# Two halves of the adaLN sums, h modulated on ScalarE, two projection tiles in turn

## What is computed

```python
mod = silu(c) @ ada_w + ada_b                      # c: 1024, ada_w: 1024 x 3072
shift, scale, gate = split(mod, 3)
h = rmsnorm(x, norm_g) * (1.0 + scale) + shift     # x: 1024 x 1024, f32
z = h @ w_in                                       # 1024 x 2760
xr, gr, q, k, v, ga, qi, ki, wi = split(z)
y_r = rg_lru(conv(xr)) * silu(gr)                  # 512 channels
y_a = dsa_attention(q, k, v, qi, ki, wi) * silu(ga)   # index scores, top 256 keys per query
x = x + gate * (concat(y_r, y_a) @ w_out)
out = rmsnorm(x, final_g)
```

## Time and profile before

| | |
|---|---|
| median of 3 runs | 621.33 us (620.89 to 621.44) |
| the profiled execution's own time | 619.93 us |
| its span, first to last instruction | 618.1 us |
| mean granted TensorE clock | 0.926 of full |
| busy: TensorE, VectorE, ScalarE, GpSimd | 87%, 71%, 61%, 38% of the span |

### The profile page before, as it was taken

How to read it: one execution, slowest core, us unless ns; L and a number is a source line. 1 busy time by engine, 2 the same in 40 slices (tenths; PEclk the granted TensorE clock), 3 DMA queues, 4 the chain that set the end, 5 groups by cost and what they waited for, 6 DMA issues and landing times.

```text
span 618.1 us, 8029 instructions
## 1 busy us (share of the span) xinstructions
PE 535.4 (87%) x2676; PEld 444.8 (72%) x2676; DVE 439.5 (71%) x992; ACT 377.4 (61%) x679; POOL 233.5 (38%) x195
## 2 busy tenths in 40 slices
PE   1459989998999999999999526489999999999994
PEld 1346868777787777778888415478889999888873
DVE  5987386885999889898697886854475666664522
ACT  6513236453499999987898555554466666656531
POOL 5150862352344274677642003740402030313322
PEclk9859999998999999999999855569999999999999
DMA  8967342430112111135550420110011000101011
GB/s 335 418 206 266 105 118 53 102 85 18 36 34 69 34 36 34 35 103 137 140 133 0 177 96 0 68 36 2 8 61 43 28 36 34 41 30 69 0 69 68
DMA packets 16457, 51.96 MB, mean 84 GB/s; under 512 B 4000, under 2 KB 5024, under 8 KB 15392
## 3 DMA queue, kind: packets, MB, share of 16 engines
q1 hardware_dynamic: 16416, 51.45, 26.3%
HBM read 37.81 MB, written 4.19 MB: 68 GB/s over the span
## 4 chain that ended last, share of the span: by engine, by line
PE 68%; DVE 11%; DMA 7%; POOL 5%; ACT 4%; issue 3%; SPq 2%; DVEq 0%; POOLq 0%; ACTq 0%
PE pair L1373 30%; PE pair L1470 13%; PE pair L1492 6%; PE pair L1505 5%; DMA ada<-in_ada_w 4%; PE pair L1448 3%; PE pair L1449 2%; DMA qs<-half_lo 2%; PE pair L1422 2%; DVE rank L1156 2%; PE pair L1514 2%; PE pair L1413 2%; PE pair L1414 2%; DVE tie L1158 1%; POOL half_lo L726 1%
## 5 line engine op out<-in xcount | busy, mean ns | idle before, releaser
L1373 PE MATMUL pair<-h_hi,w_hi 128*128 128x512 f32 (+1 forms) x352 | 114.4, 407 | 1.6 <-DVE h_lo L1064 1.5
L1373 PE MATMUL pair<-h_lo,w_hi 128*128 128x512 f32 (+1 forms) x352 | 109.8, 393 | 0.0
L1373 PE MATMUL pair<-h_hi,w_lo 128*128 128x512 f32 (+1 forms) x352 | 109.0, 391 | 0.0
L1298 DVE TENSOR_TENSOR pt_lo<-pair,pt_hi 128x512 fp32r<-128x512 f32 (+3 forms) x96 | 50.5, 554 | 71.1 <-ACT pt_hi L963 70.5
L858 ACT ACTIVATE bias_sb<-score_sb,tinies 128x1024 bf16<-128x1024 f32 (+2 forms) x93 | 95.7, 1032 | 3.2 <-DVE tinies L1109 3.1
L696 POOL TENSOR_SCALAR w_hi<-w_raw 128x1024 fp32r<-128x1024 f32 (+1 forms) x22 | 29.4, 1339 | 136.3 <-PE pair L1373 120.5
L1373 PEld LDWEIGHTS pair<-h_hi,w_hi 128*128 128x128 f32 (+1 forms) x352 | 65.0, 188 | 19.0 <-issue 6.2
L1373 PEld LDWEIGHTS pair<-h_lo,w_hi 128*128 128x128 f32 (+1 forms) x352 | 66.0, 188 | 15.5 <-issue 0.8
L1373 PEld LDWEIGHTS pair<-h_hi,w_lo 128*128 128x128 f32 (+1 forms) x352 | 65.6, 186 | 15.4 <-issue 0.7
L1095 DVE TENSOR_SCALAR_CACHE_REDUCE bias_sb<-score_sb,tinies 128x640 bf16<-128x640 f32 (+2 forms) x93 | 72.6, 802 | 0.9
L781 POOL TENSOR_TENSOR x_res<-q_free,x_res 128x512 f32<-128x512 f32 x14 | 18.1, 1296 | 121.0 <-DVE q_free L1269 121.0
(11 more groups left out here) (195 smaller groups left out, 1254.2 us busy)
## 6 DMA issues: line engine op xcount, KB each, us to landing
w_raw<-in_w_tiles SPq DMA_DIRECT2D x21, 512.0 KB, 3.5
ada<-in_ada_w SPq DMA_DIRECT2D x8, 1024.0 KB, 18.4
x_sb<-in_x SPq DMA_DIRECT2D x8, 512.0 KB, 7.1
ada_g<-in_ada_w SPq DMA_DIRECT2D x8, 512.0 KB, 4.5
qs<-half_hi SPq DMA_DIRECT2D x16, 256.0 KB, 3.6
qs<-half_lo SPq DMA_DIRECT2D x16, 256.0 KB, 4.4
wo_raw<-in_w_out SPq DMA_DIRECT2D x8, 512.0 KB, 6.4
x_res<-in_x SPq DMA_DIRECT2D x8, 512.0 KB, 3.3
```

Of the source, the lines that this page charges most:

```text
L1298: nc.vector.tensor_tensor(pt_lo[:, 4 * b:4 * b + nc4, hh, :], psum[use % 2][:, 0:nc4 * P].rearrange("p (c q) -> p c q", q=P), f32(pt_hi[:, ...
L1373: ins = nc.tensor.matmul(psum[banks[half]][0:width, :], w[b][:, k, 0:width], hh[:, k, half * HALF:(half + 1) * HALF], start=(k == 0 and p ...
```

## The change

`MOD_GROUPS` becomes two equal halves of the channel chunks, 0 to 3 and 4 to 7, and everything up to h follows them.

- SP loads slab 0, then for all eight row chunks the columns of the first half (shift and scale, 2 x 512 columns, 512 KB), then slab 1, then the same for the second half. That is sixteen loads in place of eight, with rows of 2 KB in place of 8 KB.
- VectorE sums the first half (8 operations over 1024 elements), two of the second, forms shift and scale of the first, sums two more, and then takes `low_half(k)` and a sum in turn; then shift and scale of the second half and four more `low_half`.
- ScalarE modulates: h_hi directly from `xt` with Identity, bias and scale, then `xt` in place.
- TensorE does the first column sums, then ksteps of tile 0 and tile 1 in turn for each chunk, with the second column sums ahead of chunk 3.
- `FIRST_US` goes from 46 to 37.

```diff
-MOD_GROUPS = [(0, 3), (3, KC)]
+MOD_GROUPS = [(0, KC // 2), (KC // 2, KC)]
-FIRST_US = 46.0
+FIRST_US = 37.0
...
-            for k in range(KC):
-                sp.dma_start(ada[k][:, :], ada_w[k * P:(k + 1) * P, 0:2 * D]).then_inc(ada_in[k], 16)
-                if k >= KC - 2:
-                    load_slab(k - (KC - 2))
+            for n in range(2):
+                load_slab(n)
+                for k in range(KC):
+                    src = ada_w[k * P:(k + 1) * P, 0:2 * D].rearrange("p (b m) -> p b m", b=2)
+                    sp.dma_start(ada[k][n][:, :, :], src[:, :, n * (D // 2):(n + 1) * (D // 2)]).then_inc(ada_in[k][n], 16)
...
             for k in range(KC):
-                act.wait_ge(h_full, k + 1)
-                nc.scalar.activation(h_hi[:, k, :], xt[:, k, :], ACT.Copy).then_inc(h_hi_ok, 1)
+                act.wait_ge(mod_ok, k // (KC // 2) + 1)
+                act.wait_ge(xt_act, 2 * KC)
+                shift, scale = mod[:, k:k + 1], mod[:, 8 + k:9 + k]
+                nc.scalar.activation(h_hi[:, k, :], xt[:, k, :], ACT.Identity, bias=shift, scale=scale).then_inc(h_hi_ok, 1)
+                act.wait_ge(h_hi_ok, k + 1)
+                nc.scalar.activation(xt[:, k, :], xt[:, k, :], ACT.Identity, bias=shift, scale=scale).then_inc(h_full, 1)
...
+            def accumulate(k, n):
+                g0, g1 = MOD_GROUPS[n]
+                v_acc = acc[:, :].rearrange("p (b m) -> p b m", b=2)[:, :, g0 * P:g1 * P]
+                dve.wait_ge(ada_in[k][n], 16)
+                if k == 0:
+                    dve.wait_ge(c_ok, 1)
+                    nc.vector.tensor_scalar(v_acc, ada[k][n][:, :, :], c_act[:, k:k + 1], None, ALU.mult).then_inc(acc_ok[n], 1)
+                else:
+                    dve.wait_ge(acc_ok[n], k)
+                    nc.vector.scalar_tensor_tensor(v_acc, ada[k][n][:, :, :], c_act[:, k:k + 1], v_acc, ALU.mult, ALU.add).then_inc(acc_ok[n], 1)
+            def modulation(n):
+                g0, g1 = MOD_GROUPS[n]
+                dve.wait_ge(mod_ps, n + 1)
...
+            def low_half(k):
+                dve.wait_ge(h_full, k + 1)
+                nc.vector.tensor_tensor(h_lo[:, k, :], xt[:, k, :], f32(h_hi[:, k, :]), ALU.subtract).then_inc(h_lo_ok, 1)
             for k in range(KC):
...
+                accumulate(k, 0)
+            accumulate(0, 1)
+            accumulate(1, 1)
+            modulation(0)
+            accumulate(2, 1)
+            accumulate(3, 1)
+            for k in range(KC // 2):
+                low_half(k)
+                accumulate(KC // 2 + k, 1)
+            modulation(1)
+            for k in range(KC // 2, KC):
+                low_half(k)
...
+            mod_sums(0)
             for k in range(KC):
-                kstep(0, k)
-                if k >= KC // 2:
-                    kstep(1, k - KC // 2)
-            for k in range(KC // 2, KC):
-                kstep(1, k)
+                if k == KC // 2 - 1:
+                    mod_sums(1)
+                for j in range(2):
+                    kstep(j, k)
```

More of the change, by code:

```diff
@@ L351, in layer_kernel @@
         R_H = region(65536)
-        ada = [sb(f"ada{k}", R_H + 8192 * k, [P, 2048]) for k in range(KC)]
+        ada = [[sb(f"ada{k}_{n}", R_H + 32768 * (k // 4) + 16384 * n + 4096 * (k % 4), [P, 2, D // 2]) for n in range(2)] for k in range(KC)]
         h_hi = sb("h_hi", R_H, [P, KC, S], F32R)
@@ L479, in layer_kernel @@
         x_in = [sem(f"x_in{t}") for t in range(NT)]
-        ada_in = [sem(f"ada_in{k}") for k in range(KC)]
+        ada_in = [[sem(f"ada_in{k}_{n}") for n in range(2)] for k in range(KC)]
         w_in_s = [sem(f"w_in{b}") for b in range(2)]
@@ L496, in layer_kernel @@
         mod_ps = sem("mod_ps")
-        acc_ok = sem("acc_ok")
+        acc_ok = [sem(f"acc_ok{n}") for n in range(2)]
+        mod_ok = sem("mod_ok")
         h_full = sem("h_full")
@@ L1065, in _ @@
-            dve.wait_ge(h_hi_ok, KC)
-            nc.vector.tensor_tensor(h_lo[:, KC - 1, :], xt[:, KC - 1, :], f32(h_hi[:, KC - 1, :]), ALU.subtract).then_inc(h_lo_ok, 1)
+            def accumulate(k, n):
[8 more added lines that the diff above has]
+                    nc.vector.scalar_tensor_tensor(v_acc, ada[k][n][:, :, :], c_act[:, k:k + 1], v_acc, ALU.mult, ALU.add).then_inc(acc_ok[n], 1)
@@ new lines, in modulation @@
+            def modulation(n):
+                g0, g1 = MOD_GROUPS[n]
+                dve.wait_ge(mod_ps, n + 1)
+                v_mod, v_ps, v_b = (t.rearrange("p (b k) -> p b k", b=2)[:, :, g0:g1] for t in (mod[:, :], psum[7 - n][:, 0:16], sm[:, 16:32]))
+                link(nc.vector.tensor_tensor(v_mod, v_ps, v_b, ALU.add))
+                nc.vector.scalar_tensor_tensor(mod[:, 8 + g0:8 + g1], mod[:, 8 + g0:8 + g1], 1.0, sm[:, 8 + g0:8 + g1], ALU.add, ALU.mult).then_inc(mod_ok, 1)
+            def low_half(k):
+                dve.wait_ge(h_full, k + 1)
+                nc.vector.tensor_tensor(h_lo[:, k, :], xt[:, k, :], f32(h_hi[:, k, :]), ALU.subtract).then_inc(h_lo_ok, 1)
@@ L1336, in _, with mod_sums @@
                     ins.then_inc(xt_ps, 1)
-            for g, (g0, g1) in enumerate(MOD_GROUPS):
-                pe.wait_ge(acc_ok, len(MOD_GROUPS) * (KC - 1) + g + 1)
+            def mod_sums(g):
+                g0, g1 = MOD_GROUPS[g]
+                pe.wait_ge(acc_ok[g], KC)
                 for n in [*range(g0, g1), *range(KC + g0, KC + g1)]:
```

## The result

The changed kernel takes **625.11 us** (median of 20 runs, 619.11 to 626.53). The kernel before took 620.13 in the 20 runs beside it (619.45 to 621.44). The ratio is **1.0057, with an interval of 1.0036 to 1.0078**: some 3.5 us slower by the ratio, which goes with the means (623.8 against 620.3), and 5.0 by the medians. The forecast, 623.9 against 621.33, was a ratio of 1.0041.

A forecast was written before the change was run, and what follows sets the result against it. TensorE was taken as the bound, with the start of idx 0 as the measure. Terms -0.7 (tile 0), +1.1 (GpSimd) and +2.1 (clock) gave +2.5, called 2.6: 621.33 + 2.6 = 623.9 us, range 619.8 to 626.8.

The forecast's parts named there:

- The sign: Whole kernel: slower at 0.62, against faster 0.17 and same 0.21; the sum was +2.5, called 2.6.
- tile 0's end: End of tile 0's projection on TensorE: at 62.2, 0.7 earlier (bounds 60.7 to 64.5).
- GpSimd's term: From tile 0's end to idx 0, beside earlier gate sums: 23.4 us against 22.3, +1.1 (bounds 21.3 to 24.5).
- The first matmul: Head of TensorE: starts at 36.2, 9 us earlier; the measure is when idx 0, the first index matmul, starts.
- The rate of 2 KB rows: Loads of ada_w: 385 GB/s, so the first halves take 10.9 us and land at 26.0.
- Six ksteps from cold: TensorE's head: from 36.2, ten matmuls cold, two warm, four ksteps, to 46.4; second column sums 2.0, to 48.4.
- The clock: TensorE at idx 0: starts cold after waiting 6 us, 3.6 to 4.5 us at half rate, a loss of 2.1.
- the fall at 141: Rival: the fall of TensorE's clock at 141, after a wait of 3.20, goes away; -1.8, 622.1; chance 0.17.
- The loads: Rival: gaps behind held issues or slow 2 KB rows delay the head; +2 to +4 more, 626 to 628; chance 0.12.
- shut out: Rival: GpSimd's five parts each wait a whole gate sum, 12.4 instead of 10.3; idx 0 2.1 later, 626.0; chance 0.02.
- The faster rival: Rival: gate sums do not slow GpSimd; idx 0 at 81.5, TensorE waits under 2 us, stays warm; -3.7, 617.6; chance 0.14.
- E0: The time at which tile 0 ends; in the kernel before, idx 0 is at E0 + 22.3.

The follow-up runs named there:

- kept warm: Extra matmuls nobody reads put in TensorE's waits: on the changed kernel 621.05 us, ratio 1.0013; on the kernel before 618.20 us, ratio 0.9969.

## Why the prediction was right

The sign was forecast for the right reason: tile 1 and the second half of the sums take tile 0's lead, idx 0 does not come earlier, and cold starts of TensorE come on top. The size is in part luck. The terms were -0.7, +1.1 and +2.1; the profile has +1.9 for tile 0's end, -0.1 for GpSimd and +2.7 behind idx 0, 4.5 in all. So tile 0's end was 2.6 us too early in the forecast (64.8 against 62.2, outside my bounds of 60.7 to 64.5), the excess in GpSimd's term took 1.2 of it back, and the agreement in size holds only for the ratio, which the five low times pull down: by the medians the loss is 5.0 and not 2.6.

**Right by its own steps.**
- The sign, and the size by the ratio: +2.6 forecast (1.0041), 1.0057 measured with an interval that holds the forecast. The first matmul was not the measure: 6.7 us earlier there became 1.8 later at idx 0. That an earlier idx 0 shortens the time is seen in the spans of the profiles kept warm; no run has a lower median for it.
- The rate of 2 KB rows (385 against 389 GB/s) without gaps. The 15 us more that the fit of the Trainium skill's page "DMA: Bandwidth & Descriptors", section "Anatomy of one DMA — SWDGE (gpsimd) path", made for DMAs that GpSimd issues, would give by my estimate if loads of 512 KB did not overlap are not seen.
- Six ksteps from cold and then the column sums: 10.2 us forecast, 48.69 - 38.43 = 10.3; the sums themselves 2.0 against 1.84; four chunks at 11.1 against 66.1 - 54.89 = 11.2.
- TensorE, not VectorE, decides the second column sums (VectorE's last sum ends at 46.7, they start at 48.69), and tile 0 gives its lead to tile 1. From the first matmul to tile 0's end it is 26.4 us instead of 17.7: four more ksteps of tile 1 (5.5), the column sums (1.8) and the wait for chunk 4 (1.5) make 8.8 of the 8.7.
- Kept warm, TensorE reaches idx 0's place at 82.99, which is tile 0's end (65.9) + 17.1 where I had 17.2, and would then wait 5.1 us.

**Wrong in its terms:**
- *Tile 0's end*: -0.7 forecast, +1.9 in the profile. The first half of VectorE's sums ends 2.2 late. Of this 1.3 is that eight sums lie 1.39 apart and not 1.23 (1.28 for one, 0.11 to the next, since each waits for the one ahead), and 0.7 that split 0 and the start of split 1 now lie beside the first and the last of them on GpSimd (1.74 and 1.80 from start to start). Identity with bias and scale adds 0.8: it takes 1.24 us where I took Copy's 1.06, twice for the first chunk of each half. Shorter column sums and small operations gave 0.4 back. Identity is 17% over Copy where I had allowed "perhaps a tenth", and the sums end at 30.3 where I had bounded them at 29.2.
- *GpSimd*: +1.1 forecast, -0.1 measured. Split 3 took 4.9 us and not 5.8: the first gate sum (71.57), with one operand, left w_hi alone, and the sums with two started at 72.52, 0.6 after the first w_lo, which took 1.60. Before, split 3 took 4.1 and had waited 0.8 for tile 1. The rule of the Trainium skill, page "SBUF — State Buffer", section "Who interferes with whom", that whoever comes second waits for the whole instruction, is not borne out in size: parts beside gate sums took 2.27 and alone 1.28, so 1.0 more and not a sum of 1.28.
- *The clock*: the mechanism was right and its place was partly another. I had one cold start at idx 0 after 6 us. The trace has falls at 70.0 and at 87.0, which make one loss between them, since what runs cold while idx 0 cannot start costs nothing. From idx 0 to idx 36 the change loses 3.17 - 1.83 = 1.3 us (2.1 forecast). From there to the end it loses another 1.3, of which 1.0 lies behind the v transposes, where the clock falls at 274.8. I did not have that fall: the kernel before has full clock there (1.00 from 268 to 280). Moving all after idx 0 by 2 to 3 us was not "the same work in the same order" for the clock.

**Of the rivals**: the fall at 141 stayed (at 145.0). The loads were not late. GpSimd was neither free nor shut out. The faster rival let the clock hold behind a wait of "under 2 us"; its own sum, E0 + 19.3 against E0 + 17.2, is 2.1, and after 2.04 us the clock fell. The five runs of twenty at 619.1 to 620.3 show how near the changed kernel comes to "same" in executions with a higher mean clock: what they have in their traces was not seen, since the profiled execution is one of the thirteen, and which of the falls they lack stays open. They are also 1.0 us faster than the change kept warm (medians 620.05 and 621.05), so falls of the clock need not be all that they lack. The 3.65 us at idx 0 in the two warm profiles stand against 2.85 in the medians; single executions scatter by this much, since the first matmul on h lies up to 0.9 us apart in profiles with the same head, and the clock's rise after it adds as much.

## What to carry to other kernels

An earlier first matmul is worth nothing if the tile that releases the next slow chain does not end earlier; here that is tile 0, and the chain is GpSimd's to the first index matmul. Moving half of a reduction behind the first chunks puts its fixed parts (column sums, two small operations, the first chunk's latency) in the middle of dense work; the kernel before has them twice too, but both sets of column sums stand ahead of its first matmul on h. Before judging a small loss, fill TensorE's waits with matmuls nobody reads: it takes the clock out of most of the comparison (here from 50 to 350 us), and by itself it made the kernel before 0.3% faster.

## What the runs showed of the hardware that was not expected

- How long TensorE stood idle does not tell alone whether its clock falls. After 2.52 us of waiting it held (kernel before, idx 0), and even after 3.14 (kernel before with the gate sums early, idx 36 at 142.50: 1.00 from 142 to 150). After 2.04 us it fell (changed kernel, idx 0), as it did 1.4 us behind a wait of 2.47 (at 70.0) and 1.1 us behind one of 1.50 with eight 64-wide transposes after it (at 274.8).
- One-column matmuls run at the clock's rate too: 16 in 3.57 us at half clock, in 1.84 at full.
- A sum on VectorE that waits for the one just ahead of it costs 0.11 us more than its own 1.28; two independent halves of 512 elements take 0.67 each (9.35 for 14), 1.34 for both, against 1.39.
- ScalarE's Identity with a scale and bias per partition takes 1.24 us for 1024 elements where Copy takes 1.06.
- Loads of 512 KB with rows of 2 KB ran at 389 GB/s, those of 1 MB with rows of 8 KB at 423: 1.7 us over ada_w's 8.4 MB, as the kernel before with halved loads showed (38.39 against 36.67). Which of the two halvings does it is not separated.
